# The inverse of the softmax sums of a prompt attention, moved from VectorE's reciprocal to a power of minus one on POOL, with all engine orders laid out again

## What is computed

```python
def masked_softmax(s, mask):
    s = jnp.where(mask, s, -jnp.inf)
    m = jnp.max(s, axis=-1, keepdims=True)
    e = jnp.exp(s - m)
    return e / jnp.maximum(jnp.sum(e, axis=-1, keepdims=True), 1e-30)
...
o = gate[..., 0, None] * o_c + gate[..., 1, None] * o_s + gate[..., 2, None] * o_w
```

## Time and profile before

| | |
|---|---|
| median of 3 runs | 1703.75 us (1701.75 to 1704.07) |
| the profiled execution's own time | 1706.4 us |
| its span | 1704.7 us |
| granted TensorE clock over the span, mean | 0.971 of full speed |
| the prompt attention, from its first query transposes to the first output projection | about 476 to 787 us of the span |

### The profile page before, as it was taken

How to read it: one execution, slowest core, us unless ns; L and a number is a source line. 1 busy time by engine, 2 the same in 40 slices (tenths; PEclk the granted TensorE clock), 3 DMA queues, 4 the chain that set the end, 5 groups by cost and what they waited for, 6 DMA issues and landing times.

```text
span 1704.7 us, 26443 instructions
## 1 busy us (share of the span) xinstructions
PE 1615.1 (95%) x9869; PEld 1393.6 (82%) x9869; DVE 807.4 (47%) x1506; ACT 498.6 (29%) x1037; POOL 496.2 (29%) x506
## 2 busy tenths in 40 slices
PE   7999999999789999998999999999999999999995
PEld 7989998785576677775779998899988999889993
DVE  5673211423258898984352335433354333543337
ACT  6222222222037666773242111111111111111112
POOL 3472332615035444452122113111131111311112
PEclk9999999999869999999999999999999999999998
DMA  6140225328220000005002111121111211121102
GB/s 204 51 155 26 78 65 123 101 77 224 51 72 4 7 5 4 1 1 185 1 0 75 38 38 37 52 59 37 37 37 55 56 37 37 37 58 52 37 12 100
DMA packets 100717, 99.08 MB, mean 58 GB/s; under 512 B 7801, under 2 KB 86234, under 8 KB 100538
## 3 DMA queue, kind: packets, MB, share of 16 engines
q1 hardware_dynamic: 82266, 78.67, 15.4%
q0 software_dynamic: 4880, 11.91, 2.5%
q10 hardware_dynamic: 13488, 7.41, 1.6%
HBM read 90.81 MB, written 11.34 MB: 60 GB/s over the span
## 4 chain that ended last, share of the span: by engine, by line
PE 86%; DVE 8%; ACT 2%; issue 2%; POOL 1%; DMA 0%; ACTq 0%; POOLq 0%; DVEq 0%
PE bankpair L2294 10%; PE bankpair L2296 10%; PE bankpair L2295 10%; PE bankpair L2321 5%; PE bankpair L2322 5%; PE bankpair L2323 5%; PE bankpair L1017 4%; PE bankpair L365 4%; PE bankpair L366 4%; PE bankpair L369 4%; PE bankpair L1834 3%; PE bankpair L1803 2%; PE bankpair L1914 2%; PE bankpair L1915 2%; PE bankpair L1916 2%; PE bankpair L1805 2%
## 5 line engine op out<-in xcount | busy, mean ns | idle before, releaser
L2294 PE MATMUL bankpair<-h2T_high,w_high 128*128 128x344 f32 x1056 | 337.6, 320 | 0.0
L2296 PE MATMUL bankpair<-h2T_high,w_low 128*128 128x344 f32 x1056 | 337.1, 319 | 0.0
L2295 PE MATMUL bankpair<-h2T_low,w_high 128*128 128x344 f32 x1056 | 337.1, 319 | 0.0
L2345 POOL TENSOR_TENSOR w_low<-work,w_high 128x1024 fp32r<-128x1024 f32 x44 | 105.3, 2415 | 566.6 <-ACT w_high L2340 566.4
L2424 DVE TENSOR_TENSOR x_all<-x_all,bankpair 128x512 f32<-128x512 f32 (+1 forms) x396 | 251.6, 683 | 1.6
L2410 DVE TENSOR_TENSOR kT_space<-kT_space,bankpair 128x344 f32<-128x344 f32 x66 | 33.9, 513 | 451.4 <-ACT kT_space L2358 451.4
L2358 ACT ACTIVATE kT_space<-bankpair 128x344 f32<-128x344 f32 x66 | 30.3, 459 | 624.1 <-PE bankpair L2296 624.1
L2294 PEld LDWEIGHTS bankpair<-h2T_high,w_high 128*128 128x128 f32 x1056 | 198.6, 188 | 2.9
L2295 PEld LDWEIGHTS bankpair<-h2T_low,w_high 128*128 128x128 f32 x1056 | 198.1, 188 | 0.8
L2296 PEld LDWEIGHTS bankpair<-h2T_high,w_low 128*128 128x128 f32 x1056 | 198.4, 188 | 0.0
L365 PE MATMUL bankpair<-win_high,h_high 128*128 128x256 f32 (+2 forms) x648 | 187.8, 290 | 0.4 <-POOL win_low L537 0.4
(11 more groups left out here) (311 smaller groups left out, 2811.6 us busy)
## 6 DMA issues: line engine op xcount, KB each, us to landing
work<-in_w_gate SPq DMA_DIRECT2D x22, 512.0 KB, 5.0
work<-in_w_up SPq DMA_DIRECT2D x22, 512.0 KB, 6.3
work<-in_w_down SPq DMA_DIRECT2D x22, 512.0 KB, 3.7
x_all<-in_x_prompt SPq DMA_DIRECT2D x15, 512.0 KB, 11.7
work<-in_w_in SPq DMA_DIRECT2D x7, 1024.0 KB, 5.2
work<-in_cache_kv_cmp POOLq DMA_DIRECT2D x32, 128.0 KB, 3.5
work<-in_cache_kv_cmp SPq DMA_DIRECT2D x32, 128.0 KB, 3.5
work<-in_state_win_kv ACTq DMA_DIRECT2D x16, 256.0 KB, 5.0
```

What stands on the lines that cost most here:

```text
L2294: pe.matmul(out, wh, high, start=(k == 0), stop=False)
L2295: pe.matmul(out, wh, low, start=False, stop=False)
L2296: ins = pe.matmul(out, wl, high, start=False, stop=(k == KD - 1))
L2345: pool.tensor_tensor(w_low[s][x], w_raw[s][x], w_high[s][x].bitcast(F32), ALU.subtract).then_inc(gu_low, 1)
```

## The change

The reciprocal on VectorE goes, and its semaphore with it. In its place POOL raises the sums to the power of minus one with a tensor-by-tensor operation, against a small tile that holds -1.0 in two columns, once per request, and waits for the result through its chain before it scales. The piece is called RQ; it waits for ACT's release of the request's bank pair, as the reciprocal did. In the planner RQ takes POOL, a length of 0.3 us and a rank just ahead of RS; VectorE's RS, planned with 0.15 us, is gone. As the lists are made by the planner, the orders of all engines are laid out again.

```diff
+    minus_one = sb("minus_one", [P, 2])
...
         chain.link(pool.memset(minus_half[:, :], -0.5))
+        chain.link(pool.memset(minus_one[:, :], -1.0))
...
-            "dve": ("QT", "CV", "QK", "RS", "T", "SELT", "CN", "CI", "OT", "OBN", "OBT"),
-            "pool": ("QL", "QT", "RS", "CG", "OBQ", "WS"), "dma": ("QL",)}
+            "dve": ("QT", "CV", "QK", "T", "SELT", "CN", "CI", "OT", "OBN", "OBT"),
+            "pool": ("QL", "QT", "RQ", "RS", "CG", "OBQ", "WS"), "dma": ("QL",)}
...
-                    t = add("dve", "RS", ask, 0.15, t)
+                    t = add("pool", "RQ", ask, 0.3, t)
                     for r in ask[1]:
                         add("pool", "RS", (n, (r,)), 0.1 + 0.0011 * cols, t)
...
+            elif name == "RQ":
+                n, heads = a
+                kind = steps[n][2]
+                wait_taken(pool, ("QK", a))
+                own = slice(heads[0], heads[-1] + 1)
+                chain.link(pool.tensor_tensor(inv_sum[kind][:, own], row_sum[kind][:, own], minus_one[:, 0:len(heads)], ALU.pow))
             elif name == "RS":
                 n, r = a[0], a[1][0]
                 i, g, kind = steps[n]
-                pool.wait_ge(inv_sum_ready, q_at[ask_of(n, r)[1]] + 1)
...
-            elif name == "RS":
-                n, heads = a
-                kind = steps[n][2]
-                wait_taken(dve, ("QK", a))
-                own = slice(heads[0], heads[-1] + 1)
-                dve.reciprocal(inv_sum[kind][:, own], row_sum[kind][:, own]).then_inc(inv_sum_ready, 1)
```

More of the change, by code:

```diff
@@ L1708, in build_program @@
     s_taken = [sem("s_taken0"), sem("s_taken1")]
-    max_ready, inv_sum_ready, p_scaled = sem("max_ready"), sem("inv_sum_ready"), sem("p_scaled")
+    max_ready, p_scaled = sem("max_ready"), sem("p_scaled")
     pt_ready, pt_high_ready, pt_low_ready = sem("pt_ready"), sem("pt_high_ready"), sem("pt_low_ready")
@@ L2033, in stage4_pool @@
                 i, g, kind = steps[n]
-                pool.wait_ge(inv_sum_ready, q_at[ask_of(n, r)[1]] + 1)
                 col = 3 * (NR * g + r) + branch_gate[kind]
                 p = p_of[kind][:, r, 0:P * len(key_tiles(i, kind))]
-                pool.tensor_scalar(p, p, gate[:, i, col:col + 1], inv_sum[kind][:, r:r + 1], ALU.mult, ALU.mult)\
-                    .then_inc(p_scaled, 1)
+                pool.tensor_scalar(p, p, gate[:, i, col:col + 1], inv_sum[kind][:, r:r + 1], ALU.mult, ALU.mult)                    .then_inc(p_scaled, 1)
             elif name == "OBQ":
```

## The result

The changed kernel took 1714.35 us (median of 4 runs, 1713.64 to 1716.37), the kernel before 1703.91 beside it. The ratio is 1.0064, with a 95% interval of 1.0049 to 1.0080: 10.4 us slower, beyond the forecast range of 1696 to 1710 us and on the side that had a chance of 0.28.

A forecast was written before the change was run, and what follows sets the result against it. TensorE, 86% of the chain, was taken as the bound, nearly full in attention beside VectorE; -4.3 us of relief, +3.6 on POOL and zero for the orders gave -0.7, so 1703.0 us, range 1696.0 to 1710.0.

The forecast's parts named there:

- the side that had a chance of 0.28: Whole kernel slower by over 0.2% because POOL's queue becomes the wait of the first two query tiles; chance 0.28.
- The new orders: All five queues laid out again, attention pieces swap places: taken as zero, with 3.4 us either way for the range.
- The bound from the clock alone: Attention: a swapped place at full clock takes 1.7 us less; one or two places give 1.7 to 3.4 us either way.
- What it takes away: Attention, VectorE loses 96 reciprocals: 4.3 us faster, two fifths of an upper bound of 10.7 us.
- The lower bound of 0.7 us: Least relief from removing VectorE's reciprocals: the ten that lie on the chain itself, 0.7 us in all.
- What it adds: Attention, POOL gets 96 powers that delay scalings and transposes in the first two query tiles: 3.6 us slower.
- the lateness worked out: First two query tiles: fourth scalings passing the start of their transposes, 5.2 us with 0.57 us powers, 9.2 with 0.77.
- the upper bound of 9.2: Most that POOL's powers could cost: 9.2 us of late scalings in eight steps, with 0.77 us per two-head power.
- The late tiles: The 24 steps from 530 us on: POOL needs 1.53 us per scaling, one every 1.56; 0.2 us of lateness together.
- The sum: Whole kernel: -4.3 + 3.6 = -0.7 us, moving the median of 1703.75 to 1703.0 us.
- The third rival: First two tiles wait for POOL's queue: price 7 to 9 us, less 1 to 3 relief, some +6, 1709.8; chance 0.28.
- the signs named ahead: TensorE's idle time from 560 to 760 us falls below 13.0 us; before 530 us transposes often wait for POOL.

The follow-up runs named there:

- the run shown: Kernel before, only the orders laid out again with 0.18 us instead of 0.15 as the planner's length of VectorE's reciprocal: 1717.34 us, ratio 1.0093.

## Why the prediction was wrong, point by point

**The new orders** are the first step that failed: "I take zero and keep 3.4 for the range." It treated a new layout as a coin that falls either way. It did not show itself as one here: with the reciprocal left on VectorE, the orders of the change cost 0.22%, 4 us, and two other layouts of the unchanged kernel cost 9 and 16. All three are on one side. Three are few, but the order of before was the best of those tried, so an edit that makes the planner lay out again may well start with a loss, as this one did. The bound from the clock alone, 1.7 us a place, was far too small for this: in the run shown, waits for bank pairs alone grew by 5.5 us.

**What it takes away**, -4.3 us, is the second: it came out at about nothing, and its reason was wrong. Taking 64 reciprocals from VectorE where it is 90% busy moved the time by +0.06% (from 1 us faster to 3 us slower). The lower bound of 0.7 us, from the ten reciprocals on the chain, was the one to take. A busy share of 90% was read as a queue that everybody waits for; the wait rows of VectorE itself show it waiting for the others as soon as it is relieved.

**What it adds**, +3.6 us, was right for the first two tiles, in mechanism and, under the orders of the change, in size: the transposes wait 3.4 us more for the scalings (4.0 against 0.6), and the runs put the early powers at some 4 us. The burst grows by 1.6 us where 1.7 were predicted, and the power took 565 and 721 ns. The reason for the size is not borne out, though: the plan was to hide half of the lateness worked out (5.2 to 9.2 us), but under the old orders, which have no power in their plan, the waits grew by about as much (4.4 against 0.6); they were shorter, 2.3 us, only in the run with the orders of the change and the powers of tiles 0 and 1 alone. And that the old orders lost 10 us, near the upper bound of 9.2, is luck: most of it goes not with waits but with a lower granted clock (last section), which the term does not have.

**The late tiles** are the third step that failed. Taken as free at a pace of 1.53 us against 1.56, they cost nothing clear of noise under the old orders, but some 2 us under the new, where the compressed scores wait 2.9 us for POOL's cast. The prediction named this cast among the work that stands behind a power and put no wait of TensorE's on it.

The factor of about two that the Trainium skill gives for elementwise work with two inputs on GpSimd ("GPSIMD Engine Reference", section "Engine selection") is not borne out for this small operation: 565 ns against 154 is 3.7.

**The sum** as measured, from the columns of the change: 4 us for the orders, 4 for the early powers, 2 for the late ones, and no relief, 10 of the 10.4 us, each with an uncertainty of 2 to 3. The third rival had the right sign and the right place for the early powers, but its +6 was put together from a price of 7 to 9 us, where they cost some 4, and a relief of 1 to 3 that did not come; it had neither the orders nor the late cast. Of the signs named ahead, one failed (TensorE's idle time from 560 to 760 us stayed at 13.0 us) and one held only in part: before 530 us the transposes wait for POOL in two places, 0.9 us in all, and from 530 to 560 us in four, 3.1 us in all.

What stays open: why the three other layouts are slower, how the waits for POOL go together with a lower clock, and whether a layout exists in which the power costs nothing. No run was faster than the kernel before.

## What to carry to other kernels

When an edit passes through a planner, price the new layout by relaying the unchanged program a few times first; here that alone moved the time by 9 and 16 us, more than any term of the forecast. Take a relief at what lies on the chain, not at a share of the engine's busy time, when another engine is as full: here TensorE, busy for 187 of 200 us. And look for the burst: POOL, busy for 137.6 of 311 us before the change, set the pace in the few microseconds in which several of its pieces stand in a row and TensorE waits behind them.

## What was not expected of the hardware

The price of the power by columns is not a line: 565 ns for one column, 721 for two, 1183 for four, so 156 ns for the second column and 231 for each of the next two. And a loss can go with the clock. In the run with the power in tiles 0 and 1 under the old orders, the stretch from 480 to 560 us reads

```profile
480.00:560.00 80.00, 71.55 (x363) 56.64 (x364) 47.66 (x86) 39.72 (x123) 42.50 (x69) 0.72 0.05 18
```

with a mean granted clock of 0.72 where it was 0.81, so more of it was spent at the lower of the two levels, 1.2 GHz. TensorE's busy time fell by 2.6 us only, yet it got through 363 matmuls in place of 425. An estimate from the two rows: 2.6 us more of standing still and 80 x (0.81 - 0.72) = 7.2 us of clock make 9.8 us, about the whole loss of that run.

This is not one odd execution. Over the whole span the mean granted clock was 0.969 to 0.972 in this run's six executions and 0.971 to 0.977 in the 29 of the kernel before beside it, in the mean 0.9705 and 0.9743; (0.9743 - 0.9705) x 1702 = 6.5 us is an estimate of the clock's part of the 10 us by these. And from 480 to 560 us the profiles of the three runs with the power in tiles 0 and 1 under the old orders show 0.69 to 0.72, that with the cheap multiplication there 0.78, and those of the kernel before and the four runs that leave these tiles their reciprocal under these orders 0.80 to 0.85. The change itself kept 0.81 there and lost its time standing still instead. How the waits for POOL bring the clock down was not tested by itself.
